# Stick-breaking logits: two heads per matmul through a zero-padded k^T, and both heads' masks in one matmul

## The reference, cut to what matters

```
z      = q @ k^T * 64**-0.5                        # per head, 128 queries x keys
brk    = where(key < query, softplus(z), 0)
remain = reversed cumulative sum of brk over later keys
a      = where(key < query, exp(log_sigmoid(z) - remain), 0)
o      = a @ v                                     # then o @ w_out
```

## Time and profile before

| what | value |
|---|---|
| median of 3 runs | 1044.78 us (1044.02 to 1060.37) |
| span of the profiled execution, first to last instruction | 1042.4 us |
| PE busy, share of the span | 98% |
| DVE, ACT, POOL busy | 55%, 46%, 3% |
| granted TensorE clock, mean | 0.998 |

### The profile page before, as it was taken

One profiled execution on the slowest core, in us unless ns is written; L12 is line 12 of the kernel. 1 busy time (PEld: TensorE's weight loads), 2 busy tenths in 40 slices (PEclk: granted clock), 3 DMA queues, 4 the chain that ended last, 5 costly groups with the idle time before them and its releaser, 6 DMA issues.

```text
span 1042.4 us, 12747 instructions
## 1 busy us (share of the span) xinstructions
PE 1025.2 (98%) x4790; PEld 833.1 (80%) x4790; DVE 573.6 (55%) x624; ACT 477.7 (46%) x522; POOL 33.6 (3%) x63
## 2 busy tenths in 40 slices
PE   6999999999999999999999999999999999999998
PEld 5777888888888777888888888777888888888887
DVE  4674754454473555655445475664446675445453
ACT  5544634434455454634434454444534354434432
POOL 1010100000000000000000003000000000000000
PEclk9999999999999999999999999999999999999999
DMA  8631656555555322556556546344534457556551
GB/s 259 259 120 40 238 177 201 175 189 197 185 195 167 114 89 83 194 191 198 183 181 200 180 164 211 121 152 126 187 131 167 156 165 239 184 179 201 182 181 40
DMA packets 113590, 177.31 MB, mean 170 GB/s; under 512 B 7696, under 2 KB 75920, under 8 KB 113552
## 3 DMA queue, kind: packets, MB, share of 16 engines
q1 hardware_dynamic: 112400, 172.80, 50.0%
q0 software_dynamic: 864, 3.41, 1.0%
q10 hardware_dynamic: 288, 0.59, 0.2%
HBM read 175.72 MB, written 1.05 MB: 170 GB/s over the span
## 4 chain that ended last, share of the span: by engine, by line
PE 93%; DVE 3%; DMA 1%; POOL 1%; SPq 1%; issue 0%; ACT 0%; ACTq 0%; DVEq 0%
PE psum L1293 27%; PE psum L1295 27%; PE psum L1294 27%; PE psum L1350 4%; PE psum L1370 2%; PE psum L1576 2%; DVE low L896 1%; PE psum L1372 1%; PE psum L1578 1%; DMA raw<-in_ev_w_in 1%; DVE arena L1090 1%; DMA cst<-consts 1%; DVE small L1089 1%; PE psum L1390 1%; PE psum L1598 1%; POOL head_rs L531 0%
## 5 line engine op out<-in xcount | busy, mean ns | idle before, releaser
L896 DVE TENSOR_TENSOR low<-raw,high 128x2048 fp32r<-128x2048 f32 (+1 forms) x163 | 369.6, 2268 | 308.0 <-ACT high L570 307.6
L570 ACT ACTIVATE high<-raw 128x2048 fp32r<-128x2048 f32 (+1 forms) x163 | 308.9, 1895 | 257.3 <-PE psum L1295 250.8
L1293 PE MATMUL psum<-high,xh 128*128 128x512 f32 x912 | 362.7, 398 | 0.0
L1295 PE MATMUL psum<-high,xl 128*128 128x512 f32 x912 | 355.9, 390 | 0.0
L1294 PE MATMUL psum<-low,xh 128*128 128x512 f32 x912 | 355.2, 390 | 0.0
L1295 PEld LDWEIGHTS psum<-high,xl 128*128 128x128 f32 x912 | 171.2, 188 | 36.6
L1293 PEld LDWEIGHTS psum<-high,xh 128*128 128x128 f32 x912 | 171.3, 188 | 35.0 <-issue 2.0
L1294 PEld LDWEIGHTS psum<-low,xh 128*128 128x128 f32 x912 | 171.5, 188 | 33.3
L1293 PE MATMUL psum<-high,gh 128*128 128x512 f32 x240 | 93.6, 390 | 0.0
L1295 PE MATMUL psum<-high,gl 128*128 128x512 f32 x240 | 93.4, 389 | 0.0
L1294 PE MATMUL psum<-low,gh 128*128 128x512 f32 x240 | 93.4, 389 | 0.0
(11 more groups left out here) (144 smaller groups left out, 683.3 us busy)
## 6 DMA issues: line engine op xcount, KB each, us to landing
raw<-in_ffn_w SPq DMA_DIRECT2D x132, 512.0 KB, 4.2
raw<-in_w_in SPq DMA_DIRECT2D x52, 512.0 KB, 4.6
raw<-in_od_w_qkv SPq DMA_DIRECT2D x24, 512.0 KB, 4.7
raw<-in_w_ffn_gate SPq DMA_DIRECT2D x22, 512.0 KB, 4.0
raw<-in_w_ffn_up SPq DMA_DIRECT2D x22, 512.0 KB, 4.9
raw<-in_w_ffn_down SPq DMA_DIRECT2D x22, 512.0 KB, 3.9
raw<-in_ev_w_in SPq DMA_DIRECT2D x12, 512.0 KB, 6.3
raw<-in_ev_w_out SPq DMA_DIRECT2D x8, 512.0 KB, 4.4
```

The lines of the kernel that those rows point to most:

```text
L570: nc.scalar.activation(high[:, n % RING, 0:cols], raw[:, n % RING, 0:cols], ACT.Copy).then_inc(high_ready, 1)
L896: nc.vector.tensor_tensor(low[:, n % RING, 0:cols], raw[:, n % RING, 0:cols], high[:, n % RING, 0:cols].bitcast(F32), ALU.subtract).then_i ...
L1293: nc.tensor.matmul(out, sh, wh, start=start, stop=False, skip_group_check=True)
L1295: return nc.tensor.matmul(out, sl, wh, start=False, stop=stop, skip_group_check=True)
```

## The change

`k^T` goes into a new tile `o_kp` with an extra index e for the head: for e = 0 the rows 64 to 127 stay zero, for e = 1 the rows 0 to 63. With it one 128-row matmul per query block gives the logits of both heads, over 2 x 128 keys for t = 0 and 2 x 256 keys for t = 1, and one matmul with the mask repeated by a zero step masks both heads. The zeros are written once by POOL. ACT copies each transposed k chunk in two halves of 64 rows. The logits lie in PSUM as 512 columns of bank 4 (t = 1) and 256 of bank 5 (t = 0), and the tiles `o_stay`, `o_beta`, `o_later` and `o_a` follow this order. The result of a @ v of the odd pairs moves to columns 256 to 511 of bank 5. To make room, `o_tok` lies in `xn`.

```diff
-        o_tok = take(4 * 512).rearrange("p (b t n) -> p b t n", b=2, t=NT)
+        o_tok = xn[:, :, :].rearrange("p t (b n) -> p b t n", b=2)
-        o_kT = take(8 * SEQ).rearrange("p (f j t) -> p f j t", f=2, j=4)
+        o_kp = take(8 * 2 * SEQ).rearrange("p (f j e t) -> p f j e t", f=2, j=4, e=2)
...
@@ POOL, after the row statistics of the first feed-forward norm
                 if e == 1:
+                    nc.gpsimd.memset(o_kp, 0.0).then_inc(o_kp_zeroed, 1)
                     pool.wait_ge(pooled_ready, 1)
                     pool.dma_start(cst[:, CONST_COLS["bands"][0]:DECAY_AT], consts[:, DECAY_AT:]
...
@@ ACT, copy_T
-                    dst = (o_qT, o_kT)[f][:, half, :, t * P:(t + 1) * P]
-                    nc.scalar.activation(dst, bank(QK_T_BANK[half, f] + t).rearrange("p (j n) -> p j n", j=4), ACT.Copy
-                                         ).then_inc(qkvT_copied, 1)
+                    if f == 0:
+                        nc.scalar.activation(o_qT[:, half, :, cols], src, ACT.Copy).then_inc(qkvT_copied, 1)
+                    else:
+                        act.wait_ge(o_kp_zeroed, 1)
+                        for e in range(2):
+                            rows = slice(e * HD, (e + 1) * HD)
+                            nc.scalar.activation(o_kp[rows, half, :, e, cols], src[rows], ACT.Copy).then_inc(qkvT_copied, 1)
...
@@ DVE, stick_weights: still four scans, the same lengths
+                    for t in range(NT):
+                        c0, c1 = pair_cols(t, e)
+                        stay = o_stay[:, c0 + 1:c1][:, ::-1]
...
@@ PE, stick_z
-                for e in range(2):
-                    rows = slice(e * HD, (e + 1) * HD)
-                    q, k = o_qT[rows, half, j, :], o_kT[rows, half, j, :]
-                    for t, (c0, c1) in enumerate(((0, P), (P, TRI))):
-                        nc.tensor.matmul(bank(Z_BANK + e, c0, c1), q[:, t * P:(t + 1) * P], k[:, 0:c1 - c0], start=True, stop=False,
-                                         skip_group_check=True)
-                        ins = nc.tensor.matmul(bank(Z_BANK + e, c1 - P, c1), identr[:], strictr[:], start=False, stop=True,
-                                               skip_group_check=True)
-                ins.then_inc(z_ready, 1)
+                q, k = o_qT[:, half, j, :], o_kp[:, half, j, :, :]
+                z0 = bank(Z_BANK + 1, 0, SEQ).rearrange("p (e n) -> p e n", e=2)
+                z1 = bank(Z_BANK).rearrange("p (e n) -> p e n", e=2)
+                mask = strictr[:, :].unsqueeze(1).to_broadcast([P, 2, P])
+                nc.tensor.matmul(z0, q[:, 0:P], k[:, :, 0:P], start=True, stop=False, skip_group_check=True)
+                nc.tensor.matmul(z0, identr[:], mask, start=False, stop=True, skip_group_check=True)
+                nc.tensor.matmul(z1, q[:, P:SEQ], k, start=True, stop=False, skip_group_check=True)
+                nc.tensor.matmul(z1[:, :, P:SEQ], identr[:], mask, start=False, stop=True, skip_group_check=True
+                                 ).then_inc(z_ready, 1)
@@ PE, stick_aT: waits on the copies counted anew
-                    pe.wait_ge(qkvT_copied, 4)
+                    pe.wait_ge(qkvT_copied, 6)
                 if p == 1:
-                    pe.wait_ge(qkvT_copied, 6)
+                    pe.wait_ge(qkvT_copied, 8)
                 if p == 3:
-                    pe.wait_ge(qkvT_copied, 8)
+                    pe.wait_ge(qkvT_copied, 12)
```

More of the change, by code:

```diff
@@ L53, with pair_cols @@
 TRI = P + SEQ
+PAIR = 2 * TRI
+def pair_cols(t, e):
+    return (e * SEQ, (e + 1) * SEQ) if t else (2 * SEQ + e * P, 2 * SEQ + (e + 1) * P)
 UNIT = 2048
@@ L273, in program @@
         take = Carve()
-        o_tok = take(4 * 512).rearrange("p (b t n) -> p b t n", b=2, t=NT)
+        o_tok = xn[:, :, :].rearrange("p t (b n) -> p b t n", b=2)
         o_qT = take(8 * SEQ).rearrange("p (f j t) -> p f j t", f=2, j=4)
-        o_kT = take(8 * SEQ).rearrange("p (f j t) -> p f j t", f=2, j=4)
+        o_kp = take(8 * 2 * SEQ).rearrange("p (f j e t) -> p f j e t", f=2, j=4, e=2)
         o_v = take(4 * 512).rearrange("p (f t n) -> p f t n", f=2, t=NT)
[L278 to L281, removed]
+        o_stay = take(PAIR)
+        o_beta = take(PAIR)
+        o_later = take(PAIR)
+        o_a = take(PAIR)
         A_RING = 4
@@ L311, in program @@
         masks_ready = sem("masks_ready")
+        o_kp_zeroed = sem("o_kp_zeroed")
         half_ready = sem("half_ready")
@@ L349, in bank, with two_banks @@
             return psum[:, b, c0:c1]
+        def two_banks(b):
+            return psum[:, b:b + 2, :].rearrange("p b n -> p (b n)")
         def slot_tile(ring, n, k, cols):
@@ L416, in pv_bank, with pv_out @@
             return (A_T_BANK, Z_BANK)[p % 2]
+        def pv_out(p, rows):
+            if pv_bank(p) == Z_BANK:
+                return psum[rows, Z_BANK + 1, SEQ:512].rearrange("p (t n) -> p t n", t=NT)
+            return psum[rows, A_T_BANK:A_T_BANK + 2, TRI:512]
         block = ctx.enter_context(nc.Block())
@@ L767, in copy_T @@
                     act.wait_ge(qkvT_ready, 4 * half + 2 * f + t + 1)
-                    dst = (o_qT, o_kT)[f][:, half, :, t * P:(t + 1) * P]
-                    nc.scalar.activation(dst, bank(QK_T_BANK[half, f] + t).rearrange("p (j n) -> p j n", j=4), ACT.Copy
-                                         ).then_inc(qkvT_copied, 1)
+                    cols = slice(t * P, (t + 1) * P)
+                    src = psum[:, QK_T_BANK[half, f] + t, :].rearrange("p (j n) -> p j n", j=4)
+                    if f == 0:
[5 more added lines that the diff above has]
+                            nc.scalar.activation(o_kp[rows, half, :, e, cols], src[rows], ACT.Copy).then_inc(qkvT_copied, 1)
             def stick_sigmoids(p):
                 act.wait_ge(z_ready, p + 1)
-                z = psum[:, Z_BANK:Z_BANK + 2, 0:TRI]
+                z = two_banks(Z_BANK)[:, 0:PAIR]
                 if p:
@@ L790, in stick_out @@
                 act.wait_ge(sbv_ready, p + 1)
-                b = pv_bank(p)
-                nc.scalar.activation(mh[:, p, :].rearrange("p (t n) -> p t n", t=NT), psum[:, b:b + 2, TRI:512], ACT.Copy
+                nc.scalar.activation(mh[:, p, :].rearrange("p (t n) -> p t n", t=NT), pv_out(p, slice(0, P)), ACT.Copy
                                      ).then_inc(sbv_high, 1)
@@ L1141, in stick_weights @@
                 else:
-                    dve.wait_ge(ones_set, 1)
+                    dve.wait_ge(ones_set, 2)
                 for e in range(2):
-                    for c0, c1 in ((0, P), (P, TRI)):
-                        stay = o_stay[:, e, c0 + 1:c1][:, ::-1]
-                        nc.vector.tensor_tensor_scan(o_later[:, e, c0:c1 - 1][:, ::-1], stay, stay, 1.0,
+                    for t in range(NT):
+                        c0, c1 = pair_cols(t, e)
+                        stay = o_stay[:, c0 + 1:c1][:, ::-1]
+                        nc.vector.tensor_tensor_scan(o_later[:, c0:c1 - 1][:, ::-1], stay, stay, 1.0,
                                                      ALU.mult, ALU.min).then_inc(later_ready, 1)
@@ L1156, in stick_out @@
                 dve.wait_ge(sbv_high, p + 1)
-                b = pv_bank(p)
-                nc.vector.tensor_tensor(ml[:, p, :].rearrange("p (t n) -> p t n", t=NT), psum[:, b:b + 2, TRI:512],
+                nc.vector.tensor_tensor(ml[:, p, :].rearrange("p (t n) -> p t n", t=NT), pv_out(p, slice(0, P)),
                                         mh[:, p, :].bitcast(F32).rearrange("p (t n) -> p t n", t=NT), ALU.subtract
                                         ).then_inc(sbv_low, 1)
-            nc.vector.memset(o_later.rearrange("p e (b n) -> p e b n", n=P)[:, :, 0:TRI // P:2, P - 1], 1.0).then_inc(ones_set, 1)
+            nc.vector.memset(o_later[:, SEQ - 1:2 * SEQ:SEQ], 1.0).then_inc(ones_set, 1)
+            nc.vector.memset(o_later[:, 2 * SEQ + P - 1:PAIR:P], 1.0).then_inc(ones_set, 1)
             for u in range(16):
@@ L1564, in stick_z @@
                 if j == 0:
-                    pe.wait_ge(qkvT_copied, 4 * half + 4)
+                    pe.wait_ge(qkvT_copied, 6 * half + 6)
                     pe.wait_ge(masks_ready, 3)
@@ L1596, in stick_aT @@
                 for e in range(2):
-                    for j in range(3):
-                        ins = nc.tensor.transpose(bank(A_T_BANK + e, j * P, (j + 1) * P), o_a[:, e, j * P:(j + 1) * P], ident)
+                    starts = pair_cols(0, e)[0], pair_cols(1, e)[0], pair_cols(1, e)[0] + P
+                    for j, c0 in enumerate(starts):
+                        ins = nc.tensor.transpose(bank(A_T_BANK + e, j * P, (j + 1) * P), o_a[:, c0:c0 + P], ident)
                 ins.then_inc(aT_ready, 1)
@@ L1610, in stick_pv @@
                     v = [o_v[:, half, b, (2 * j + e) * HD:(2 * j + e + 1) * HD] for b in range(NT)]
-                    dst = [psum[e * HD:(e + 1) * HD, pv_bank(p) + t, TRI:512] for t in range(NT)]
```

(2 more changed lines are left out.)

## The result

The changed kernel takes 1031.53 us (median of 10 runs, 1028.77 to 1042.04); the kernel before 1044.99 (median of 10, the three listed above among them, 1043.21 to 1060.37). The ratio is 0.9867, 95% interval 0.9839 to 0.9895: 1.3% faster. Executions more than 1.5% above the fastest of their kernel (1060.37 here, 1047.09 in one experiment) are left out of the ratios. The gain is within the 2% that I had named as no clear change, but the interval excludes 1, so ten runs each do tell it from nothing. The profiled execution took 1032.42 us, 1.8 more than its span.

The account below looks back on a forecast made before the run. PE, busy 98% of the 1042.4 us span, was taken as the bound. Eight pairs saving 1.56 us each give 12.5 us, with nothing booked elsewhere: 1044.8 - 12.5 = 1032.3 us, range 1029.5 to 1038.5.

Parts of the forecast that it names:

- The bound: Whole kernel: PE, busy 98% of the 1042.4 us span, sets the time, so what PE sheds the span sheds.
- What the logits before are made of: Logits of a head pair, 3.12 us: eight changes of array shape each expose a 0.20 us weight load, 1.6 us together.
- The price after: New logits of a pair: 0.43 + 0.11 + 0.86 + 0.11 = 1.51 us, booked as 1.56, saving 1.56 a pair.
- The allowance: New logits: 0.05 us per pair for one place where a short matmul does not quite hide the next load.
- The sum: Whole kernel: eight pairs save 12.5 us, span 1029.9 us, median of runs 1032.3 us, 1.2% less.
- The covers: Added ACT copies, later sigmoids and POOL's zeroing: waiting time already there hides them, so nothing is booked.
- The cover at unit 9: Two more ACT copies of k^T end at 369.83, 1.0 us before PE needs them for pair 3's transposes.
- The table load: ACT before the first sigmoid: loading until 334.74 delays it 0.5 us after z, within 1.7 us of slack; costs nothing.
- A: New logits: every float32/fp32r weight change still exposes 0.20 us, so half stays and time is 1038.3 us; chance 0.15.
- C: ACT's longer queue delays unit 9 copies or sigmoids about 0.5 us per pair; price 4 us, time 1036.3; chance 0.05.
- D: POOL's slow zeroing at 113.6 us holds DVE; PE loses its length M minus 5.4 us, slower than before; chance 0.02.
- B: Old logits: heads already run side by side and pairing gives that up; no time of its own, no chance stated.

Follow-up runs that it names:

- side by side order: Kernel before with only the logits' order changed, per query block both heads' 64-row matmuls, then both masks: 1035.28 us, ratio 0.9886 to before.
- four_then_masks: Kernel before, unpadded, with each pair's logits reordered to all four float32 matmuls, heads alternating, then four masks: 1031.85 us, ratio 0.9848 to before.

## Why the prediction was right

- *The bound.* PE's list set the time before and does so after. Over the changed kernel and the five experiments on the logits, eight times the price of a pair with the product behind it gives the differences of the medians to within 1.3 us. Right.
- *What the logits before are made of.* The step on which all rested was that eight loads of 0.20 lie bare in each pair because the shape changes eight times. Adding the shape back to the changed kernel gave 0.19 to 0.20 at each place, taking it out of the kernel before removed the six inside the pair and left the first and the last. Shown from both sides, and a load that stands alone in the timeline lasts 0.18 or 0.19. The Trainium skill, TensorE: Matmul & The Clock Gate, part 3, "The mechanism", has loads overlap only when the row group differs, though the same section also names a background weight buffer as a way ahead. Here all loads of the new group are in one row group, and the load at 342.18 overlaps 0.59 us of passes; the measurement decides against the rule as I read it in the prediction.
- *The price after.* Expected 0.43 + 0.11 + 0.86 + 0.11 with 0.05 of allowance, measured 0.43 + 0.12 + 0.86 + 0.12. The allowance was for a mask that doesn't cover the next load; masks of 256 columns do cover it. At pair 1 the saving was 1.58 with 0.05 behind it, over the stage 1.59 a pair, against my 1.56. The pass over 512 columns, the repeated mask and the gap in k^T do cost their columns and nothing else.
- *The sum.* 12.5 us expected in the span, 12.7 found in the stage, 11.8 in the span, because this execution was 0.9 us behind before the change's first instruction. The median of the runs, 1031.53, lies 0.8 below the forecast 1032.3, and that it lies so near is in part luck: the span came out 0.7 above my 1029.9, and the 2.4 us that I put between span and median, one execution's span against the median of three runs, was 0.9 this time (an execution's own time is 1.8 above its span). The scatter of the clock is as large as these.
- *The covers.* A half-height copy lasts as long as a full one, as priced (592 ns against 596), but the four took 2.44 us where my 1.09 + 2 x 0.49 makes 2.07. The cover at unit 9 was 0.7 us, not 1.0, and it held. The table load, 1.28 us from 334.43 on, pushed the first sigmoid to 335.73, 0.5 us after z was ready at 335.21. No wait of PE came of either.
- *Rivals.* A (loads stay bare, 1038.3) fell with the pair at 1.53. C (a wait) left no entry. D (POOL's memset holds DVE) fell with the run of five memsets; the memset's 3.5 us would have been below its 5.4 in any case. Of B I wrote that it gave no time of its own; the side by side order shows that it had one: the overlap of the heads was there to be had, unused, and with it the kernel before reaches the changed one without padding. I had seen it in the index scores and had not drawn that conclusion.

## What to carry to other kernels

Look at the rows and columns that each matmul takes of the array, in order of issue. Where 64-row matmuls take turns with 128-row ones, each turn costs about 0.20 us here, and padding with zeros to 128 rows pays although half of the multiplications are by zero; grouping matmuls of one shape, with heads in opposite row halves next to each other, pays as much and needs no zeros. Then look for short matmuls: here an fp32r mask of 256 columns covered the next weight load and one of 128 left 0.05 us of it bare; nothing between was tried.

## What the runs showed of the hardware that was not expected

- Between runs of one kernel the granted clock is not the same. Below is the same stretch of the changed kernel and, in the second row, of `four_then_masks`, whose work before 100 us is the same but for a few places in memory. It lies in the first block's softmax, after PE had waited 1.3 us for DVE (columns as in the earlier trace rows):

```profile
74.00:78.00 4.00, 4.00 (x10) 2.75 (x11) 1.24 (x5) 1.68 (x8) 0.00 (x0) 0.50 0.83 262
...
74.00:78.00 4.00, 4.00 (x19) 2.79 (x18) 0.96 (x5) 0.92 (x4) 0.00 (x0) 1.00 0.75 250
```

  The changed kernel had the 1.2 GHz level there, 0.50, and 10 passes in 4 us; `four_then_masks` had 1.00 and 19 passes, also after a wait of 1.3 us. From the start of the softmax logits to POOL's statistic that makes 42.5 us against 39.5. Over its ten runs the changed kernel's span goes with its clock: 1027.0 and 1027.1 at 1.000, 1030.6 at 0.997, 1040.2 at 0.985. Most of the scatter of this kernel goes with the clock. The two kernels with padded softmax attentions had 0.999 or 1.000 in all eight executions; whether the padding does that was not tried, nor what decides the level.
- A memset of POOL costs 0.86 ns per column of float32 over 4096 columns, and 17.88 us of it beside DVE left every DVE operation beside it as long as in the changed kernel, to within 0.02 us.
